# A hybrid decoder step on one core: the order of VectorE's row scaling and column weighting in the first norms

## The reference, cut to what matters

```python
u = rmsnorm(x, norm_mix)              # x * rsqrt(mean(x*x) + 1e-6) * norm_mix
cols = u @ w_in                       # 1024 x 4992, split among three kinds of heads
...                                   # recurrence, two kinds of attention, readouts
h = x + mix @ w_out
h = h + moe(rmsnorm(h, norm_ffn))     # 16 experts, top 2 inside the top group
y = rmsnorm(h + sigmoid(rmsnorm(h, norm_ple) @ pgw) * (p @ ppw), norm_final)
```

## Time and profile before

| | us |
|---|---|
| median of 3 runs | 1131.88 (1125.92 to 1145.94) |
| the profiled execution's own time | 1128.97 |
| its span | 1127.2 |
| mean granted clock of TensorE | 0.961 of full speed |
| TensorE busy | 1044.0 (93%) |
| VectorE busy | 372.7 (33%) |
| ScalarE busy | 249.3 (22%) |

### The profile page before, as it was taken

One profiled execution on the slowest core, in us unless ns is written; L12 is line 12 of the kernel. 1 busy time (PEld: TensorE's weight loads), 2 busy tenths in 40 slices (PEclk: granted clock), 3 DMA queues, 4 the chain that ended last, 5 costly groups with the idle time before them and its releaser, 6 DMA issues.

```text
span 1127.2 us, 11235 instructions
## 1 busy us (share of the span) xinstructions
PE 1044.0 (93%) x4079; PEld 543.2 (48%) x4079; DVE 372.7 (33%) x767; ACT 249.3 (22%) x575; POOL 80.9 (7%) x94
## 2 busy tenths in 40 slices
PE   4998999999998999888789978999999999998997
PEld 3444545544455775554354544444444444444342
DVE  4207465533126576354521251111111111100444
ACT  3125222211232332432222110100000010011354
POOL 1000000000005360000000001000000000000200
PEclk9999999998999999877889988999999999999999
DMA  5555023304347542535236085598999899886401
GB/s 196 211 199 155 17 119 131 131 1 163 130 157 238 164 163 78 183 101 173 73 108 235 20 304 195 181 351 313 335 347 347 305 348 347 297 317 268 152 20 56
DMA packets 99547, 214.92 MB, mean 191 GB/s; under 512 B 14993, under 2 KB 46180, under 8 KB 99116
## 3 DMA queue, kind: packets, MB, share of 16 engines
q1 hardware_dynamic: 86288, 185.78, 46.9%
q0 software_dynamic: 4560, 16.84, 4.1%
q10 hardware_dynamic: 8652, 11.68, 2.8%
HBM read 191.97 MB, written 41.14 MB: 207 GB/s over the span
## 4 chain that ended last, share of the span: by engine, by line
PE 81%; DVE 7%; DMA 4%; ACT 3%; SPq 2%; issue 2%; POOL 1%; ACTq 0%; DVEq 0%; POOLq 0%
PE ps L1932 15%; PE ps L2350 10%; PE ps L2380 10%; PE ps L2356 10%; PE ps L1937 6%; PE ps L2249 5%; PE ps L2445 5%; PE ps L2219 2%; PE ps L1968 2%; PE ps L1940 1%; PE ps L2014 1%; PE ps L2095 1%; PE ps L2041 1%; DMA EXPERT<-in_cache_win 1%; PE ps L2269 1%
## 5 line engine op out<-in xcount | busy, mean ns | idle before, releaser
L1932 PE MATMUL ps<-xT,EXPERT 128*128 128x512 f32 x384 | 182.9, 619 | 1.2 <-DVE EXPERT L1262 1.2
L1937 PE MATMUL ps<-EXPERT,xT 128*128 128x384 f32 (+1 forms) x384 | 118.7, 451 | 0.0
L2350 PE MATMUL ps<-EXPERT,aF 128*128 128x512 f32 x256 | 114.5, 601 | 1.3 <-DVE aF L1821 1.3
L2380 PE MATMUL ps<-EXPERT,dF 128*128 128x512 f32 x256 | 112.6, 592 | 1.6 <-ACT dF L1146 1.6
L2356 PE MATMUL ps<-EXPERT,aF 128*128 128x512 f32 x256 | 112.5, 592 | 0.0
L1932 PEld LDWEIGHTS ps<-xT,EXPERT 128*128 128x128 f32 x384 | 71.3, 197 | 81.2 <-issue 78.4
L1937 PEld LDWEIGHTS ps<-EXPERT,xT 128*128 128x128 f32 x384 | 77.7, 236 | 25.5 <-issue 3.6
L2350 PEld LDWEIGHTS ps<-EXPERT,aF 128*128 128x128 f32 x256 | 49.3, 193 | 63.6 <-issue 61.9
L2380 PEld LDWEIGHTS ps<-EXPERT,dF 128*128 128x128 f32 x256 | 48.6, 190 | 62.6 <-issue 60.7
L2356 PEld LDWEIGHTS ps<-EXPERT,aF 128*128 128x128 f32 x256 | 47.4, 190 | 53.6 <-issue 53.6
L2249 PE MATMUL ps<-EXPERT,xT 128*128 128x512 f32 x128 | 59.6, 617 | 0.8 <-ACT xT L1062 0.8
(11 more groups left out here) (417 smaller groups left out, 1170.6 us busy)
## 6 DMA issues: line engine op xcount, KB each, us to landing
EXPERT<-in_moe_w_gate SPq DMA_DIRECT2D x16, 2048.0 KB, 15.2
EXPERT<-in_moe_w_up SPq DMA_DIRECT2D x16, 2048.0 KB, 20.1
EXPERT<-in_moe_w_down SPq DMA_DIRECT2D x16, 2048.0 KB
EXPERT<-in_w_in SPq DMA_DIRECT2D x13, 1536.0 KB, 6.6
out_win_sample<-in_cache_win SPq DMA_DIRECT2D x16, 1022.0 KB
Yd<-wk ACTq DMA_DIRECT2D x16, 512.0 KB
aF<-in_cache_k_diff SPq DMA_DIRECT2D x32, 192.0 KB, 2.4
aF<-in_cache_v_diff SPq DMA_DIRECT2D x32, 192.0 KB, 2.4
```

Of the source, the lines that this page charges most:

```text
L1932: last = t.matmul(ps[:, u % 2, :], W_[:, c, c0:c0 + w], xT[:, c, 0:SEQ], start=(c == 0), stop=(c == DC - 1))
L1937: last = t.matmul(ps[:, u % 2, 0:w], rows_, W_[:, c, c0:c0 + w], start=(c == 0), stop=(c == DC - 1))
L2350: last = t.matmul(ps[:, 2 + 2 * b, :], xgT[b][:, c, :], wg_[b][:, c, :], start=(c == 0), stop=(c == DC - 1))
L2380: last = t.matmul(ps[:, 6 + hf, :], hT[b][:, c, :], wd_[b][:, c, hf * 512:(hf + 1) * 512], start=(c == 0), stop=(c == FC - 1))
```

## The change

VectorE's loop is cut into two functions, the scaling of a tile's rows and the weighting of a tile's columns, and these are issued in another order: rows 0, rows 1, columns 0, rows 2, columns 1, rows 3, columns 2, rows 4, columns 3, columns 4. The copy of the gains stays behind rows 0. The clearing of `xS` comes ahead of the weighting of the last tile's columns. No instruction is added or removed, no semaphore count is changed, and the other engines' programs are the same.

```diff
             v.memset(epsc, EPS).then_inc(S_["row_in"], 1)
-            for i in range(NT + 1):
+
+            def scaled_rows(i):
+
                 r = tile_rows(i)
                 dve.wait_ge(S_["rstd_ok"], i + 1)
                 v.tensor_scalar(XM[0:r, i, :], XM[0:r, i, :], rstd[0:r, i:i + 1], None,
                                 ALU.mult).then_inc(S_["xn_ok"], 1)
-                if i == 0:
-                    dve.wait_ge(S_["gain_pe"], 1)
-                    v.tensor_copy(gains[:], ps[:, 7, 0:27]).then_inc(S_["gain_ok"], 1)
-                    dve.wait_ge(S_["gain_ok"], 1)
+
+            def weighted_columns(i):
+
+                r = tile_rows(i)
                 dve.wait_ge(S_["xt_pe"], i + 1)
                 for h in range(2):
                     v.tensor_tensor(xT[:, 4 * h:4 * h + 4, i * P:i * P + r],
                                     ps[:, 2 * (i % 2) + h, :].rearrange("p (c t) -> p c t", c=4)[:, :, 0:r],
                                     f2(gains[:, 4 * h:4 * h + 4], r), ALU.mult).then_inc(S_["xt_ok"], 1)
+
+            scaled_rows(0)
+            dve.wait_ge(S_["gain_pe"], 1)
+            v.tensor_copy(gains[:], ps[:, 7, 0:27]).then_inc(S_["gain_ok"], 1)
+            dve.wait_ge(S_["gain_ok"], 1)
+            for i in range(1, NT + 1):
+                scaled_rows(i)
+                weighted_columns(i - 1)
             v.memset(xS, 0.0)
+            weighted_columns(NT)
             seq(v.memset(one_col, 0.0))
```

## The result

| | before | after |
|---|---|---|
| median of 20 runs each, us | 1135.38 (1125.92 to 1145.94) | 1128.59 (1117.64 to 1141.14) |
| ratio, 95% interval | | 0.9941 [0.9915, 0.9967] |
| profiled execution: own time, span, us | 1128.97, 1127.2 | 1132.49, 1130.7 |
| its mean granted clock | 0.961 | 0.948 |

The means given further on count every run of a kernel, those more than 1.5% above its fastest too; without these no gain of one kernel over another moves by more than 1.2 us.

What follows compares the result with a forecast made beforehand. Bound: a chain of waits through the first norms' tiles, VectorE and TensorE in turn, 4.01 us a step. Shift 7.8 plus clock 3.1 is 10.9 us: 1118.1 from 1128.97, 1121.0 against the median, said 1120; range 1111 to 1131.

Steps and rivals of the forecast that it cites:

- The head's mechanism: First norms: tile 1 scaled in VectorE's idle time, then VectorE sets the pace; first projection product at 17.5 instead of 25.27.
- the wait for the tables: VectorE's setup, ahead of L1266: a new wait of about 2 us for the last table's transfer, costed at nothing.
- ScalarE's eviction: Eviction of the projection's first unit, expected in time at its new place, 27.7 or 24.5, with 0.7 us or more cover.
- late statistic: Tile 2's statistic, ready at 10.34 with VectorE free at 10.37; a load 2 us late would delay weighting 1 by 2 us.
- late slab: Projection weights: slab 0 lands at 14.2 and is needed at 17.5, a cover of 3.3 us; no gain lost there.
- The first term: The shift at the head: first projection product at 17.5 instead of 25.27, worth 7.8 us.
- the clock term: Start of the projection: clock already up, so seven records are spaced 0.43 instead of 0.87 us; 3.1 us, bounds 0 and 3.1.
- ring: The repeated step per tile of the first norms, VectorE's weighting and scaling and TensorE's transposes; 4.01 us from weighting to weighting before.
- shift without the clock: Rival: the clock stays low or falls again ahead of the projection, leaving only 7.8 us, median 1123 to 1124; chance 0.25.
- The base: The starting time: profiled execution of 1128.97 us, 2.9 below the runs' median; 1118.1 from it, 1121.0 against the median, said 1120.
- The gain is swallowed: Rival: a late load of tile 2 and a DMA wait further down shrink the gain to 0 to 5 us; chance 0.16.
- rival B: Posed for the follow-up experiments: the earlier start itself costs low-clock time later, some 3 us; no chance given.

Runs made afterwards that it cites:

- two_ahead: The changed kernel with rows scaled two tiles ahead instead of one; run only once, 1129.33 us.
- after_fill: The changed kernel with 4, 4 and 8 idle transposes behind the norms' tiles 2, 3 and 4; ratio to before 0.9919 [0.988, 0.9957].
- after_again: The changed kernel run again unchanged, with a second trace; mean 1125.6 us, ratio to before 0.9928 [0.9894, 0.9961].
- before_fill: The kernel before, in the old order, with seven idle transposes behind each tile's in the norms; mean 1131.2 us, ratio to before 0.995 [0.9914, 0.9986].
- fill_and_full: The changed kernel with both idle transposes in the norms' gaps and 128-row products; mean 1118.7 us, ratio to before 0.9847 [0.979, 0.9904].
- The first sample: The changed kernel's first 20 timed runs, those of the result; mean 1128.7 us at a mean clock of 0.949.
- after_delay: The changed kernel with three clearings of an unused buffer ahead of VectorE's first scaling; mean 1136.2 us, ratio to before 1.0004 [0.9966, 1.0042].
- full_rows: The changed kernel with the eight `dst_v` products fed by 128 rows, 120 of them zero, instead of 8; mean 1117.9 us, ratio to before 0.9836.
- before_full: The kernel before with the eight `dst_v` products fed by 128 rows, 120 of them zero; mean 1129.1 us, ratio to before 0.9941 [0.9902, 0.9979].

## Why the prediction was wrong in size

**The head's mechanism was right.** VectorE without a gap from the first weighting on, the scaling of tile 1 in idle time, the wait for the tables (2.70 us, expected 2), ScalarE's eviction and the slabs in time: each as worked out. Neither a late statistic nor a late slab showed in the first trace (statistic 2 at 9.89, scaling 2 at 9.99; the margin is as thin as it was said to be, and two_ahead shows what its loss costs).

**The first term, 7.8 us, came out at 8.5** (25.2 less the mean 16.7 of three traces). Some 0.2 us of it is an earlier start of the whole chain (weighting 0 at 8.81 in the mean against 8.99), which the change does not bring. The sum had VectorE at 1.96 us a tile and TensorE at 1.98. VectorE takes 1.86, already before the clock rose (8.79 to 10.65), because weighting and scaling overlap by some 0.1 us; and in the first trace TensorE, at the high clock, never held it up. I had said that transposes at the high clock would give at most 0.1 us; they gave somewhat more, for in after_fill, where the third tile's still took 1.97 us, VectorE waited 0.20 us for them.

**The step that failed is the clock term, 3.1 us.** Measured as the lead at the third slab less the lead at the first product it is 1.0, 2.6 and -0.3 us in the three traces, 1.1 in the mean. I reasoned that the transposes would raise the clock, which held (at 10.5 us in the first trace), that TensorE would work without a real gap from 7.0 to 16.1, and that the pause of 1.4 us behind would not lower the clock. The middle part was wrong, since the rise itself thins TensorE's work: transposes of 1.09 us in a ring of 1.86, then the sample tile's 0.66, then the pause. I had named this among the rivals (shift without the clock, 0.25), but the sum took the upper bound and gave it nothing. In the six traces of a new order without delay and without idle transposes the clock fell in five, between 16.0 and 18.7 us, and stayed up in one (after_again). With the gaps filled (after_fill, before_fill, fill_and_full) it stayed up in all three. The gaps make the fall possible; whether it comes in a given run is beyond the schedule, so each of the three sizes above is in part luck.

The two together: 9.6 us at the third slab (50.36 - 40.79), against 10.9.

**The base.** I subtracted from a profiled execution that is 6 us under the kernel's mean (clock 0.961 against 0.954), and went only 2 us up from there. With the 20 runs' 1135.38 the same sum gives 1124.5. The forecast of 1120 against 1128.6 measured is thus 4.5 us of base, 1.3 us of head, and some 3 us that are left over. The first sample's lower clock has the size of this last piece.

**"The gain is swallowed"** (0.16) did not happen in the runs together. But the eighth slab's lead is only 6.8 us in the mean (291.7 of two traces less 284.9 of four with the new order), while with full rows it is 10.8. The loss is low clock in the stretch of `dst_v`, and it may not be chance. Ten traces have products of 8 rows there. In the seven whose head is early (before_fill, with the old order, among them) the stretch at the low level is 17.1 us five times, 13.7 and 6.8; in the three whose head is late (both of before, and after_delay with the new order) it is 6.8, 13.7 and 6.8. From the third to the eighth slab's load the early ones take 244.2 us in the mean, the late ones 240.8. So rival B, with some 3 us given back here for an early start, fits the traces better than chance does, but ten traces do not settle it; why the start should matter is not known.

## What to carry to other kernels

Where two engines hand a tile back and forth, look whether the second step of this tile stands ahead of the first step of the next in one engine's queue; one step ahead took 2.1 us out of each ring of 4, and two ahead lost 1.4 us again, because the queue then held ready work behind a wait. Price a gain from the clock at the state in which the new schedule leaves TensorE, not the one in which it finds it. And take the base of a forecast from many runs: one trace's mean clock tells how far off it is.

## What the runs showed of the hardware

Products that use 8 of 128 rows let the granted clock fall (0.70 to 0.91 from 236 to 264 us in ten traces) with TensorE busy 27.1 to 27.7 of 28 us; the same products with zeros on the other rows kept it at 1.00 in all three traces (full_rows, before_full, fill_and_full) and saved about 6 us in the old order and 6 to 9 in the new. The granted clock column reads 1.00 at the head until its first entry, though the records' durations show the low level (1.97 us for eight transposes, 1.09 after the rise). The run-to-run spread of one unchanged kernel, 1126 to 1147 us, goes for the most part with the mean granted clock (correlation -0.86 in 73 runs of before).
